# Loading each expert's gate and up weights in two halves, with a wait in the middle of the product

## The reference, cut to what matters

```python
def hier_moe(h, w_group, b_group, w_expert, b_expert, w_gate, w_up, w_down):
    ...  # a router picks for every token one group, and in it two experts with gates
    def run_block(args):
        xblk, e = args
        hid = jax.nn.silu(xblk @ w_gate[e]) * (xblk @ w_up[e])
        return hid @ w_down[e]
```

## Time and profile before

| | |
|---|---|
| median of 3 runs | 2631.67 us (2631.33 to 2632.38) |
| span of the profiled execution | 2630.3 us |
| PE busy | 2314.1 us, 88% of the span |
| stretch of layer 0's experts, about | 436 to 1170 us |
| stretch of layer 1's experts, about | 1871 to 2620 us |

### The profile page before, as it was taken

One profiled execution on the slowest core, in us unless ns is written; L12 is line 12 of the kernel. 1 busy time (PEld: TensorE's weight loads), 2 busy tenths in 40 slices (PEclk: granted clock), 3 DMA queues, 4 the chain that ended last, 5 costly groups with the idle time before them and its releaser, 6 DMA issues. The chain is left out here.

```text
span 2630.3 us, 36297 instructions
## 1 busy us (share of the span) xinstructions
PE 2314.1 (88%) x12366; PEld 1452.7 (55%) x12366; DVE 795.0 (30%) x2092; ACT 636.5 (24%) x1392; POOL 725.0 (28%) x1092
## 2 busy tenths in 40 slices
PE   7999995988888888869899999999588888888887
PEld 6888783433333333339799999878233333333333
DVE  4323343100000000026688878644300000000000
ACT  4000221111111111114566666642111111111111
POOL 3222111222212122113555555211122222222221
PEclk9999997999999999989999999999799999999998
DMA  5111228999999999983000000114899999999997
GB/s 133 50 49 32 80 89 320 424 423 424 424 423 424 423 424 424 424 345 103 10 9 18 10 10 1 65 48 153 362 414 415 412 415 413 415 416 414 413 415 274
DMA packets 138694, 693.02 MB, mean 263 GB/s; under 512 B 38150, under 2 KB 67846, under 8 KB 89456
## 3 DMA queue, kind: packets, MB, share of 16 engines
q1 hardware_dynamic: 114032, 658.26, 60.9%
q0 software_dynamic: 24576, 33.65, 4.4%
HBM read 679.20 MB, written 46.14 MB: 276 GB/s over the span
## 5 line engine op out<-in xcount | busy, mean ns | idle before, releaser
L1470 PE MATMUL ps<-gate_up,arena 128*64 128x384 f32 x2048 | 384.0, 532 | 87.1 <-issue 87.1
L1470 PE MATMUL ps<-arena 128*64 128x384 f32 x2048 | 384.5, 533 | 82.7 <-DMA arena<-in_exp_w_up 79.8
L1368 DVE TENSOR_TENSOR arena<-ps,xw 128x512 f32<-128x512 f32 x128 | 88.6, 692 | 930.6 <-PE ps L1460 930.5
L1470 PEld LDWEIGHTS ps<-gate_up,arena 128*64 128x64 f32 x2048 | 176.3, 148 | 263.7 <-issue 200.4
L1470 PEld LDWEIGHTS ps<-arena 128*64 128x64 f32 x2048 | 156.3, 149 | 279.7 <-issue 230.2
L1231 ACT ACTIVATE arena<-ps 128x384 f32<-128x384 f32 x128 | 62.7, 490 | 868.9 <-PE ps L1470 868.8
L959 PE MATMUL ps<-hT_split,w_split 128*128 128x512 f32 x1152 | 264.8, 391 | 8.1 <-DVE hT_split L853 8.1
L959 PEld LDWEIGHTS ps<-hT_split,w_split 128*128 128x128 f32 x1152 | 217.0, 189 | 53.7 <-DVE hT_split L853 8.7
L1489 PE MATMUL ps<-arena 128*64 128x512 f32 x960 | 226.5, 607 | 0.0
L1377 DVE TENSOR_TENSOR arena<-arena,ps 128x192 f32<-128x192 f32 x128 | 45.4, 354 | 412.9 <-ACT arena L1237 412.9
L1175 POOL DMA_INDIRECT arena<-h_rows,col_idx x128 | 136.0, 1062 | 114.6 <-POOL col_idx L1172 106.0
(11 more groups left out here) (258 smaller groups left out, 3460.1 us busy)
## 6 DMA issues: line engine op xcount, KB each, us to landing
arena<-in_exp_w_down SPq DMA_DIRECT2D x80, 1536.0 KB, 28.8
gate_up<-in_exp_w_gate SPq DMA_DIRECT2D x64, 1536.0 KB, 32.2
gate_up<-in_exp_w_up SPq DMA_DIRECT2D x64, 1536.0 KB, 36.0
arena<-in_exp_w_gate SPq DMA_DIRECT2D x64, 1536.0 KB, 31.6
arena<-in_exp_w_up SPq DMA_DIRECT2D x64, 1536.0 KB, 35.6
down<-in_exp_w_down SPq DMA_DIRECT2D x32, 1536.0 KB, 28.8
x<-in_exp_w_down SPq DMA_DIRECT2D x16, 1536.0 KB, 30.1
arena<-in_conv_w_in SPq DMA_DIRECT2D x24, 512.0 KB, 3.9
```

What stands on the lines that cost most here:

```text
L1368: dve.tensor_tensor(xT[:, slot, :, :, :].rearrange("p j h m -> p (j h) m"), c.ps[:, slot, :].rearrange("p (a m) -> p a m", m=RANKS), bc(c. ...
L1470: last_ = pe.matmul(c.ps[row:row + RANKS, 2 + slot, 0:FF], xT[:, slot, j, half, :], w_gate_up[w_slot][:, i, (4 * half + j) * FF:(4 * half ...
```

## The change

The transfer of a gate or up matrix is cut in two, by columns of a partition: the first half holds `half == 0` of the product's loop (pieces 0 to 3 of the inputs), the second the rest. For each expert the order in SP's queue is gate's first half, up's first half, gate's second half, up's second half. The first two count on the old semaphore, the last two on a new one of that slot, and `gate_and_up` waits for the new one before its ninth product pair. Nothing else is changed; the order of down of 62 and gate and up of 63 stays as it was in either layer.

```diff
     def __init__(self, c, layer):
...
         self.gate_up_loaded = [self.sems(f"gate_up_loaded{i}") for i in range(GU_SLOTS)]
+        self.second_half_loaded = [self.sems(f"second_half_loaded{i}") for i in range(GU_SLOTS)]
...
     def load_gate_up(self, sp, slot, e):
-        for i, dram in enumerate((self.gate_dram, self.up_dram)):
-            src = dram[:, bass.ds(e, 1), :].rearrange("p a f -> p (a f)")
-            sp.dma_start(self.gate_up[slot][:, i, :], src).then_inc(self.gate_up_loaded[slot], 16)
+        half = KD * FF // 2
+        for h, loaded in enumerate((self.gate_up_loaded[slot], self.second_half_loaded[slot])):
+            cols = slice(h * half, (h + 1) * half)
+            for i, dram in enumerate((self.gate_dram, self.up_dram)):
+                src = dram[:, bass.ds(e, 1), cols].rearrange("p a f -> p (a f)")
+                sp.dma_start(self.gate_up[slot][:, i, cols], src).then_inc(loaded, 16)
...
                 for half in range(2):
+                    if half == 1:
+                        pe.wait_ge(experts.second_half_loaded[w_slot], g * 8 + (32 - 8 * w_slot))
                     for j in range(4):
```

## The result

| | before | after |
|---|---|---|
| median, device us | 2631.67 (7 runs, 2628.7 to 2633.03) | 2638.83 (7 runs, 2637.45 to 2639.54) |
| ratio, 95% interval | | 1.0032 (1.0023 to 1.0041) |
| span of the profiled execution | 2630.3 | 2635.7 |

The change makes the kernel 7.2 us slower by the medians, where 10.7 were forecast; the interval of the ratio is 6 to 11 us. The profiled execution of the changed kernel is 1.4 us under its median, so the two profiles differ by 5.4 us only. The page of the changed kernel answers to the earlier trace rows: its span, the engines' busy times, the DMA share in 40 slices, and the packets of all queues.

A forecast was written before the change was run, and what follows sets the result against it. The prediction took the weight stream to bound both expert phases. Packets and completions +17.4, layer ends -3 and -4, store of rows +0.3 gave +10.7 us on 2631.67, about 2642 us, range 2633 to 2650 us.

The forecast's parts named there:

- The stream is the bound: Both expert phases: the weight stream never runs dry, so an earlier or faster PE mid-phase only lengthens the queue.
- More packets, 17.4 us: Weight stream: 16 more packets per engine and expert at 8.2 ns, plus completions: 147 ns for each of 118 experts.
- The two more completions: Per engine and expert, two more completion entries, priced at 8.2 ns each (bounds nothing and 8.2), 16 ns more.
- The ends, 3 and 4 us: Last experts: early product start gains 3 us in layer 0 (2 to 4.2) and 4 in layer 1 (3.5 to 5.3).
- the chain of scatters: Layer ends: each last scatter must wait for the one before, limiting PE's gain to 3 and 4 us.
- The beginnings, +0.3 us: Between output projection and experts, the last store of rows waits behind expert 0's gate and up: 0.15 us per layer.
- Longer issues cost nothing: SP's two more transfers per expert are hidden; the queue limit is met more often but priced at zero.
- Even: Rival: fixed packet cost at its low end and layer ends give all: +0.6 us, 2632 us; chance 0.13.
- faster: Rival: overlap hides the packets' fixed cost, ends give 7 to 9.5 us: 2622 to 2625 us; chance 0.07.
- much slower: Rival: smaller transfers leave gaps through the queue limit and engine pauses: 2653 or 2654 us; chance 0.08.

The follow-up runs named there:

- the two runs of packets alone: Kernel before with gate and up in 6144-byte, then 3072-byte packets, same three transfers, no middle wait: 2643.88 us (ratio 1.006) and 2676.06 us (1.0179).
- The run of transfers alone: Changed kernel with gate and up cut by even and odd partitions, 12288-byte packets, both waits before the first product: 2629.36 us, ratio 1.0.
- the run with halves at the beginnings: Kernel before with halves for experts 0 to 3 of each layer alone: 2625.4 us, ratio 0.9983.
- the run of packets alone: Kernel before with 6144-byte packets for gate and up through a new SBUF layout, same three transfers: 2643.88 us, ratio 1.006.

## Why the prediction was right, and where it was off

- **The stream is the bound, and PE's gain in it is given back.** Right: with the early start or without it the rate is 418 and 410 GB/s, while PE's busy share and clock differ.
- **More packets, 17.4 us.** Right in kind and size: 16.8 us in the table of markers, 8.5 ns per packet between the two runs of packets alone, where 8.2 was taken. I had left open whether it is the packet or the transfer that costs; it is the packet. The two more completions of an expert were priced at 8.2 ns each, 1.9 us in all. The run of transfers alone can't tell that from nothing by its time, and its markers show 1.5 us.
- **The ends, 3 and 4 us.** In the profile 3.3 and 4.4, and the chain of scatters took over as forecast. In the medians the two are smaller, some 4 to 5 us together, since the profiled execution of before had a long stay at the lower clock in expert 62's product (0.50 in its first 5 us, 8.36 us in all); I took 5.6 us on PE from that single case and cut it only for the scatters.
- **The beginnings, +0.3 us.** This is the step that failed. I looked there only at the store of rows behind expert 0's load, and left out the first gathers, which run beside expert 3's load. They land 0.7 to 1 us sooner, and the two beginnings came out 3.4 us shorter in the profile. With these 3.4 us the sum would have been 7.0 us.
- **Luck.** The two misses worked against each other. By the medians the ends gave some 2 us less than the 7 that I took, and the beginnings gave at least 2 us that I had not counted. The sum 16.8 - 5 - 2 is 9.8 us, and with the 5.0 us of the run with halves at the beginnings 6.8 us; the measured 7.2 and 8.6 us lie between. The runs don't divide the time more finely than that.
- **Longer issues cost nothing.** Right. SP now stands in its issues throughout the streams: from 500 to 1100 us their medians are 1.4 to 2.2 us, where 0.33 and 0.38 us were usual before, and the timeline below shows one of 6.22. Yet the engines stay full (1.02), and a matrix of up lands 26 us after its issue, more than two experts of the stream. The run with five transfers and whole packets does not test this, since its issues mostly take 0.34 to 0.55 us.

```profile
703.99 6.22 SPq L447 DMA_DIRECT2D gate_up<-in_exp_w_gate  x1
710.30 2.29 SPq L447 DMA_DIRECT2D gate_up<-in_exp_w_up  x1
```

- **The rivals.** Even, faster and much slower all needed another packet price or a price of transfers; 8.5 ns for a packet and at most some 10 ns for a transfer exclude them. The 3.5 ns at which the faster case was to begin are less than half of what the runs show. Transfers of 768 KB with whole packets, one behind another, run at 423 GB/s here, where 424 were before.

## What to carry to other kernels

Where transfers bound a phase as they do here, cutting them into shorter rows costs each packet's fixed time (8.2 to 8.9 ns in these runs) for all of them, and an earlier start of the consumer is given back by the queue (418 and 410 GB/s with it and without it); it paid only where the stream ends (some 4 to 5 us by the medians). So cut the last one or two loads, try it on those beside which short transfers must land, and leave the others whole. If more than one semaphore is wanted for a load, a cut across partitions was nearly free here (1.5 us by the markers, and no difference by the time, within 2.4 us) and one along the row was not (15.0 us for the packets alone); but it was the cut along the row that let half of the product start early here.

## What the runs showed of the hardware

- A packet costs 8.2 to 8.9 ns beside its bytes (rows of 12288 against 6144 and of 6144 against 3072 bytes), at loads that keep all 16 DMA engines busy (shares of 1.01 to 1.03).
- TensorE's granted clock rose from 0.94 to 0.99 in the streams when its wait before each product was cut in two (at 706 us of the changed kernel 1.18 and 0.89 us), and is 0.93 with the same transfers and one wait. Before expert 63 of layer 0 it waited 2.27 us and then took 7.08 us, at a granted clock of 0.66 in its first 5 us; now it waits 1.09 and 0.91 us and each half takes 2.80 us, at a granted clock of 1.00. A long wait does not always cost this: after 2.77 us in the run of packets alone the clock stayed at 1.00.
- Gathers and scatters from the other queue landed sooner beside shorter packets: layer 1's scatters in the stream 9.6 us after issue beside rows of 12288 bytes, 8.6 in the changed kernel, and 7.3 beside rows of 3072 bytes; the gathers of the whole run 8.0, 7.1 and 6.1 us, and layer 0's scatters 7.3, 7.2 and 5.9 (all medians). From the first gather of layer 0 to PE's first turn it is 1 us less. A scatter's landing from 1910 to 2560 us in the changed kernel:

```profile
DMA to landing us min/median/max: 7.8/8.6/9.7
```
